# Two first layers side by side in TensorE's columns, and moved: half ahead of the last local queries, half among the first scores

## The reference, cut to what matters

```
def compress_blocks(kv, pe, w1, w2):
    B, T, G, DH = kv.shape
    nc = (T - CMP_BLOCK) // CMP_STRIDE + 1
    idx = np.arange(nc)[:, None] * CMP_STRIDE + np.arange(CMP_BLOCK)[None, :]
    blk = kv[:, idx] + pe[:, None, :]
    blk = blk.transpose(0, 3, 1, 2, 4).reshape(B, G, nc, CMP_BLOCK * DH)
    return jax.nn.silu(blk @ w1) @ w2

kc = compress_blocks(k_cmp, pe_k, w1_k, w2_k)
vc = compress_blocks(v_cmp, pe_v, w1_v, w2_v)
```

## Time and profile before

| | |
|---|---|
| median of three runs | 1578.21 us (1571.3 to 1582.71) |
| the profiled execution, its own time | 1572.59 us |
| its span | 1570.8 us |
| TensorE busy | 97% of the span |
| mean granted clock of TensorE | 0.989 |
| nq1 to the end of nq3 | 127.63 to 145.9 us from the span's start |
| the two first layers | 145.9 to 159.86 us |
| attention1 | from 159.86 us |

### The profile page before, as it was taken

The page is one execution under the profiler, slowest core; times in us unless marked ns, Lnnn a source line. Parts: engine busy times, 40 slices in busy tenths (PEclk is TensorE's granted clock), DMA queues, the critical chain, the costliest instruction groups (busy, mean ns, idle before and its releaser), DMA issues.

```text
span 1570.8 us, 19523 instructions
## 1 busy us (share of the span) xinstructions
PE 1524.1 (97%) x7202; PEld 1209.9 (77%) x7202; DVE 822.2 (52%) x1644; ACT 617.1 (39%) x1119; POOL 350.1 (22%) x362
## 2 busy tenths in 40 slices
PE   7999999999999999999999999999999999999995
PEld 5786666788888888888888778766688888888884
DVE  4656676444455343333446787587365443443444
ACT  6433577322244232222446433566444222321223
POOL 3300455100020000000036634445531210210112
PEclk9999899999999999999999999999999999999998
DMA  5763100423232222332232662312422322233221
GB/s 195 138 153 108 51 15 1 133 95 103 85 99 89 94 94 96 104 96 94 94 101 69 162 180 89 114 48 82 147 95 81 106 96 94 94 99 103 94 81 53
DMA packets 46685, 154.11 MB, mean 98 GB/s; under 512 B 5714, under 2 KB 5906, under 8 KB 46592
## 3 DMA queue, kind: packets, MB, share of 16 engines
q1 hardware_dynamic: 41856, 137.63, 27.0%
q0 software_dynamic: 4736, 15.25, 4.4%
HBM read 142.78 MB, written 9.55 MB: 97 GB/s over the span
## 4 chain that ended last, share of the span: by engine, by line
PE 89%; DVE 5%; ACT 3%; DMA 2%; issue 2%; DVEq 0%; POOL 0%; SPq 0%; ACTq 0%
PE PSA L581 87%; PE PSA L786 2%; DMA WR<-w_in 1%; ACT AR L1313 0%; PE PSA L930 0%; DVE WL L1711 0%; DMA XT<-xT_in 0%; DVE AHL L1917 0%; ACT AHL L1362 0%; DVE AR L2390 0%; DVE AR L1917 0%; ACT WH L1241 0%; DVE AR L1740 0%; DVE ARR L1958 0%; DVE ARR L2011 0%
## 5 line engine op out<-in xcount | busy, mean ns | idle before, releaser
L581 PE MATMUL PSA<-Ah,WH 128*128 128x512 f32 x1072 | 423.2, 395 | 11.5 <-DVE Al L1720 9.1
L581 PE MATMUL PSA<-Al,WH 128*128 128x512 f32 x1072 | 418.9, 391 | 0.0
L581 PE MATMUL PSA<-Ah,WL 128*128 128x512 f32 x1072 | 418.8, 391 | 0.0
L1241 ACT CAST WH<-WR 128x1024 fp32r<-128x1024 f32 (+3 forms) x234 | 240.8, 1030 | 227.4 <-PE PSA L581 216.1
L1711 DVE TENSOR_TENSOR WL<-WR,WH 128x1024 fp32r<-128x1024 f32 (+3 forms) x207 | 254.8, 1232 | 86.7 <-ACT WH L1241 86.4
L581 PEld LDWEIGHTS PSA<-Ah,WH 128*128 128x128 f32 x1072 | 202.1, 189 | 60.4 <-issue 17.7
L581 PEld LDWEIGHTS PSA<-Ah,WL 128*128 128x128 f32 x1072 | 202.2, 189 | 42.9
L581 PEld LDWEIGHTS PSA<-Al,WH 128*128 128x128 f32 x1072 | 202.4, 189 | 41.8 <-issue 0.7
L581 PE MATMUL PSA<-Bh,WH 128*128 128x512 f32 (+1 forms) x592 | 230.4, 389 | 4.1 <-DVE Bl L1988 2.3
L581 PE MATMUL PSA<-Bh,WL 128*128 128x512 f32 (+1 forms) x592 | 229.1, 387 | 0.0
L581 PE MATMUL PSA<-Bl,WH 128*128 128x512 f32 (+1 forms) x584 | 226.5, 388 | 0.0
(11 more groups left out here) (362 smaller groups left out, 1951.4 us busy)
## 6 DMA issues: line engine op xcount, KB each, us to landing
WR<-w_in SPq DMA_DIRECT2D x228, 512.0 KB, 3.5
gt_tmp<-AR SPq DMA_DIRECT2D x16, 256.0 KB, 2.1
WR<-w_in SPq DMA_DIRECT2D x8, 384.0 KB, 3.0
XT<-scr_tmp POOLq DMA_DIRECT2D x8, 264.0 KB, 13.2
XT<-scr_tmp POOLq DMA_DIRECT2D x8, 256.0 KB, 14.2
XT<-xT_in POOLq DMA_DIRECT2D x1, 2048.0 KB, 10.0
x_tmp<-XT POOLq DMA_DIRECT2D x1, 2048.0 KB, 7.7
AHL<-gt_tmp SPq DMA_DIRECT2D x8, 256.0 KB, 3.8
```

What stands on the lines that cost most here:

```text
L581: return pe.matmul(o, l, r, start=start, stop=stop)
L1241: ac.copy(WH[p][:, 0:n], WR[j % RAW][:, 0:n]).then_inc(w_hi, 1)
```

## The change

The two first layers are no longer one behind the other. One matmul of the keys and one of the values alternate, the keys' into partitions 0 to 61 and the values' into partitions 64 to 125 of the same PSUM bank 7, so that they use different column halves of TensorE's array. The loads of w1k and w1v tiles alternate as well. The function `first_layers(tt)` does one tile of each. Parts 0 and 1 stand behind nq2, ahead of nq3; parts 2 and 3 stand in the attention, ahead of the scores of step 4. The tanh (ScalarE) and the product behind it (VectorE) move into step 4, the transposes, the second layer and its evacuation from steps 0, 2, 4 to 5, 7, 9. VectorE gathers the windows of the keys ahead of everything of ks, those of the values ahead of the low half of ks, and splits nq1, nq2 and nq3 at other places. XP and UU lie elsewhere in the on-chip memory.

```
-    t += [("w1k", i, 1024, False) for i in range(4)]
-    t += [("w1v", i, 1024, False) for i in range(4)]
+    for i in range(4):
+        t += [("w1k", i, 1024, False), ("w1v", i, 1024, False)]
...
-        C_T, C_MM, C_EV = 0, 2, 4
+        C_T, C_MM, C_EV = 5, 7, 9
...
+            def first_layers(tt):
+
+                if tt == 0:
+                    pe.wait_ge(c_xp, 32)
+                    pe.wait_ge(s_lo.sem, s_lo.end("ks"))
+                js = [tid["w1k", tt], tid["w1v", tt]]
+                for j in js:
+                    pe.wait_ge(w_ld[j % RAW], 16 * (j // RAW + 1))
+                for q in range(4):
+                    jj = 4 * tt + q
+                    for i, j in enumerate(js):
+                        last = mm(bank(7)[64 * i:64 * i + 62, 0:256], XP[i][:, 62 * jj:62 * jj + 62],
+                                  WR[j % RAW][:, 256 * q:256 * q + 256], jj == 0, jj == 15)
+                        if q == 3:
+                            last.then_inc(w_mm, 1)
...
+                    if t == 4:
+
+                        first_layers(2)
+                        first_layers(3)
...
+                if i == 2:
+                    first_layers(0)
+                    first_layers(1)
...
+            windows(0)
+            split_to(tid["nq", 1])
             for i, nm, K, L, b in ((0, "ks", KSH, KSL, 7), (1, "kw", KWH, KWL, 0)):
                 result(tid["kv", i + 2])
                 scaled(bank(b), rb)
-                split_to(tid["kv", i + 2] + 2)
+                if i == 0:
+                    windows(1)
+                    split_to(tid["nq", 2])
                 dv.wait_ge(s_hi.sem, s_hi.at(nm, 3))
                 k_low(s_lo, L, K, bank(b))
             for n, b in enumerate((1, 2, 3, 5)):
                 result(tid["nq", n])
                 scaled(bank(b), rb)
-                split_to(min(tid["nq", n] + 2, tid["nq", 3]))
+                if n == 0:
+                    split_to(tid["nq", 3])
```

More of the change, by code:

```diff
@@ L96, in build @@
     n_hi_, n_lo_, n_lop_, n_mm_ = 0, 0, 0, 0
-    for j, (name, i, n, split) in enumerate(tiles):
+    for j in sorted(range(len(tiles)), key=lambda j: tid["w1v", 1] + 0.5 if j == tid["nq", 3] else j):
+        name, i, n, split = tiles[j]
         n_mm_ += results.get(name, 1)
@@ L191, in build @@
         C1 = ARR[0:104, 20072:20080]
-        XP = [AR[:, 14944 + 992 * i:15936 + 992 * i] for i in range(2)]
+        XP = [AR[:, 16736 + 992 * i:17728 + 992 * i] for i in range(2)]
         pek = CS2[:, 0:32]
@@ L196, in build @@
         hT = [AR[:, 6656 + 128 * i:6784 + 128 * i] for i in range(2)]
-        UU, OT = AR[0:62, 18336:18592], AR[64:128, 18848:18849]
+        UU, OT = [AR[64 * i:64 * i + 62, 18720:18976] for i in range(2)], AR[64:128, 18848:18849]
         MG = v3(0, 8, 512)
@@ L1349, in attention1 @@
                         copies1(t - D_T)
+                    if t == 4:
+                        result(tid["w1v", 3])
+                        for i in range(2):
+                            ac.activation(UU[i], bank(7)[64 * i:64 * i + 62, 0:256], ACT.Tanh, scale=0.5).then_inc(c_th, 1)
                     if t < U1:
@@ L1517, in scalar_program @@
                 if i > 1:
-                    if i == 3:
+                    if i == 2:
+                        split_to(tid["nq", 2])
+                    else:
                         ac.wait_ge(g_dv.sem, g_dv.at("cl", 1))
@@ L1522, in scalar_program @@
             for i, b in enumerate((1, 2, 3, 5)):
-                split_to(min(tid["nq", i] + 2, tid["nq", 3]))
+                if i == 0:
+                    split_to(tid["nq", 3])
                 ac.wait_ge(e_z.sem, e_z.at("nq", i))
                 q_high(s_hi, QN, i, b, 0.125)
[L1526 to L1530, removed]
             attention1()
@@ L1849, in compressed @@
             def compressed(t):
+                if t == 4:
+                    for i in range(2):
+                        dv.wait_ge(c_th, i + 1)
+                        dv.scalar_tensor_tensor(out=HP[i], in0=UU[i], scalar=1.0, in1=bank(7)[64 * i:64 * i + 62, 0:256],
+                                                op0=ALU.add, op1=ALU.mult).then_inc(c_hp, 1)
                 if t == C_T + 1:
@@ L2151, in vector_program, with windows @@
                 dv.tensor_tensor(OT, bank(b)[64:128, 0:1], rb[64:128, 0:1], ALU.mult).then_inc(e_d.sem, 1)
+            def windows(n):
+                dv.wait_ge(d_kv[n], 48)
+                dv.wait_ge(d_cs1, 16)
+                for jj in range(16):
+                    dv.tensor_scalar(XP[n][:, 62 * jj:62 * jj + 62].rearrange("p (g n) -> p g n", g=2),
+                                     XKV[n][:, :, 2 * jj:2 * jj + 481:16], pek[:, 16 * n + jj:16 * n + jj + 1], None,
+                                     ALU.add).then_inc(c_xp, 1)
+            windows(0)
+            split_to(tid["nq", 1])
             for i, nm, K, L, b in ((0, "ks", KSH, KSL, 7), (1, "kw", KWH, KWL, 0)):
@@ L2447, in pool_program @@
                 pl.dma_start(X[0:64, 1, 0:1], OT).then_inc(d_kv[i], 16)
-            pl.wait_ge(c_hp, 2)
+            pl.wait_ge(c_xp, 32)
             for i in range(2):
                 pl.memset(hT[i], 0.0).then_inc(q_z, 1)
+            pl.wait_ge(e_z.sem, e_z.end("nq"))
             pl.wait_ge(d_rbo, 16)
```

## The result

The changed kernel takes 1582.2 us (median of 20 runs, 1577.3 to 1590.37), the kernel before 1574.89 us (median of 20 runs beside them, 1570.7 to 1582.71). The ratio is 1.0047, 95% interval 1.0036 to 1.0059: slower by 7.3 us. The profiled execution took 1579.36 us.

The account below looks back on a forecast made before the run. TensorE, busy for 97% of the span, was taken as the bound. Terms -4.3 - 6.65 + 7.05 + 5.15 + 1.5 = +2.75 us gave 1575.3 on the profiled execution, 1581.0 on the median; 1577 was taken between, range 1568 to 1587.

Parts of the forecast that it names:

- nq1 in time, -4.3 us: Ahead of nq1: its earlier split removes TensorE's 2.49 us gap and 1.65 us lost to the low clock; -4.3 us.
- Side by side, -6.65 us: First layers: column halves run together, taking 7.3 us in all where they took 13.95; -6.65 us.
- Rival D: First layers: column halves take turns because both write one bank; +9.4 us, 1584; chance 0.08.
- The wait for w1v1, 5.4 us: Ahead of part 1: TensorE waits 5.4 us for a load issued only after nq3's split; +7.05 with 1.65 of clock.
- Rival C: nq3 is split before TensorE reaches part 1, little is lost behind nq3; -6 us, 1571; chance 0.09.
- nq3's relay, 3.5 us: Ahead of the attention: TensorE waits about 3.5 us for nq3's scaling and halves, no longer covered; +5.15 with 1.65 of clock.
- The clock behind each gap, 1.65 us: Behind the gaps ahead of part 1 and of the attention: a stretch at 1.2 GHz costs 1.65 us each.
- The fall of the clock from 165.6 on I keep as it was: Start of the attention: the 1.2 GHz stretch from 165.6 to 171.9, costing 3.15 us, was taken as unchanged.
- Rival E: Attention's pipeline out of step with more stops, two more 1.2 GHz stretches of 3.15 us cost; +9 us, 1584; chance 0.08.
- more than two stretches at 0.50: Sign up to 285 in the profile after: more than two half-clock stretches would mean Rival E.
- In the attention, +1.5 us: Attention, steps 5 and 7: two stops of 1.1 and 1.25 us where one of 0.92 had been; +1.5 us.
- A: The whole kernel: the forecast itself, 1577 us, own range 1571 to 1584; chance 0.55.

Follow-up runs that it names:

- the pipelined kernels: Changed kernel with nq3 split early, VectorE scaling one result ahead, steps 6, 8, 14, part 1 or parts 0 and 1 behind nq3: ratios 0.9952 and 0.9947.
- the second pipelined kernel: Changed kernel with nq3 split early, VectorE scaling one result ahead, steps 6, 8, 14, parts 0 and 1 behind nq3: 1567.57 us, ratio 0.9947.

## Why the prediction was off, point by point

The sum was +2.75 us and the measured difference +7.3. The step that failed is the clock together with the stops in the attention: 1.65 us behind each of the two gaps, the fall from 165.6 "as it was", and +1.5 us for the stops. The gaps and their releasers came as forecast. But in the attention there were 4.67 us of stops and not some 2.4, and placing them apart gave back 6.6 us; and the stretches at 1.2 GHz up to the middle of the attention were 17.0 us in one execution and 34.0 in the other, against 13.6 and 6.8 before.

- **nq1 in time, -4.3 us:** right, in the trace and by itself on the chip (4.7, with 2.7 us of uncertainty).
- **Side by side, -6.65 us:** right. 32 records take 3.67 us with the last one's tail (3.65 forecast), one column half takes as long for 16, and taking the pairing away costs 6.9 us. Rival D falls.
- **The wait for w1v1, 5.4 us:** right in place, releaser and size (5.14 and 5.11). Rival C falls.
- **nq3's relay, 3.5 us:** right (3.48). What I did not see is that the relay of all tiles stood just behind the wait, so that repairing the wait alone gives 4 us and not 7.
- **The clock behind each gap, 1.65 us:** mis-sized. I took the shorter of the two cases in my rows. Behind the gap for w1v1 came 3.4 and 6.8 us at 1.2 GHz, behind nq3's relay 6.8 and 10.2, where 3.3 had been assumed behind each. By half lengths that is 5.1 us in one execution and 8.5 in the other, where I had 3.3.
- **"The fall of the clock from 165.6 on I keep as it was":** failed. It is no fixture of the program. The second execution of the kernel before did not have it, the changed kernel had it both times, and a second, of 10.2 us, once. In the first pair of profiles the clock's share even came out as forecast (+1.7), in the second it did not (+13.6 by half lengths). Rival E, at 0.08 and 1584, is nearest to what happened; its mechanism showed in one of the two executions. The sign that I gave for it was a bad one: "more than two stretches at 0.50" is met by my own forecast, which had three, and by the kernel before, which has four up to 285 (the last at 233.7, not among my rows).
- **In the attention, +1.5 us:** mis-sized. The two stops named were 1.25 and 1.30 us (1.1 and 1.25 forecast), but there is a third of 2.12 us at 180. In step 9 the evacuation of the second layer stands on ScalarE and VectorE ahead of the scores' work, and a transpose waits for ScalarE's copy. With steps 6, 8 and 14 a stop of 0.45 is left there, so the placing is the cause; as all three steps moved at once, that it is step 9 is read from the trace and not shown by itself. With it the term is +3.3 in the first pair, and 6.6 us with the clock by the experiment.
- **The number:** the sum was +2.75, a loss; by setting it between one execution and a median of three that lay 3.3 us above the later one of 20, I wrote 1577 under the 1578.21 shown and so forecast a gain by the number and a loss by the sum. On the later 1574.89 the sum is 1577.6; the time was 1582.2, inside 1568 to 1587, and within 1% as forecast. That 1577 is near 1577.6 is luck, since it came of two errors: a start 3.3 us too high and a sum cut by 4 us. "A difference under 1% can't be told from no change" was wrong too: 20 runs of each told 0.5% with an interval of 0.12% to either side. And case C's 1571 does not fit its own sum: -6 is 8.75 us under A's +2.75, which on A's scale is 1568.

What stays open: what decides the length of a stretch at 1.2 GHz, and how often each length comes. Two executions of each kernel are too few, so the split of the 7.3 us between stops and clock is argued from sums and differences of kernels, and not measured.

## What to carry to other kernels

When work is moved ahead of an in-order wait, ask what that work's own operands wait for: here a buffer was freed by the very tile that now stood behind it. A gain of TensorE columns is worth what the relays of the other engines and the loads leave of it; lay their chains out to the point where the next one binds, since mending one wait may only show another. A short stop of TensorE costs its own length and can cost clock besides (no stretch behind two stops of 0.94 us in one execution, 6.8 and 10.2 us of it around three stops in another), so several small ones at a start-up are the first thing to place apart: one line of step numbers was worth 6.6 us, of which 3.2 were the stops. And price the small part of a change by itself: here the earlier splits alone bring 4.7 us, more than half of what the pipelined kernels bring in all.

## What was not expected of the hardware

The granted clock was not a function of the program alone. The same order of instructions with the same gaps (within 0.4 us) ran 17.0 us at 1.2 GHz between the marks in one execution and 34.0 in another, 1579.36 and 1587.76 us; the kernel before had 13.6 and 6.8. The stretches were 3.4, 6.8 or 10.2 us long; at the end of the same gap of 3.5 us ahead of the attention, five executions of four kernels had 3.4 us once, 6.8 three times and 10.2 once. The changed kernel's 20 runs spread over 13.1 us and those before over 12.0, all but one of them within 6.8. That more gaps make a kernel spread wider is not shown: with gaps of 2.02 us and less, the second pipelined kernel still spread over 10.9 us in 9 runs.
